# Recurrence outputs with tokens on partitions in a two-layer mixer kernel

## The chip, the cores and the metric

One Trainium2 chip, one of its cores. The metric is the device time in microseconds of one execution: 1113.66 us, median of three runs (1113.42 to 1113.71). PE is the matmul engine, DVE the vector engine, ACT the scalar engine, SP the queue that loads weights.

## What is computed

256 tokens of width 1024 go through two blocks, each with three parallel mixers and a gated feed-forward part. Only three kinds of mixer matter here.

- The gated linear recurrences: GLA in block 1 (4 heads, values of 128), HGRN2 in block 2 (8 heads of 128). For every head `o[t] = sum over s <= t of A[t, s] v[s]`, where A holds the decayed scores. Then each head's output is normed over its 128 value channels and gated: `o * rsqrt(mean(o*o) + eps) * gain * silu(r)`.
- The mLSTM (4 heads, values of 256): `h[t] = sum A[t, s] v[s] / max(|sum A[t, s]|, exp(-m[t]))`, normed over its 256 channels, times a gain and a gate from `LO`.
- All projections are products of the normed activations with streamed weights.

All tensors are fp32. Projections are made in three passes of a rounded type (high part by high part, high by low, low by high).

## The kernel before

Weights come in 170 "pairs" of 128 x 2048 words through three slots. For each pair p SP loads `raw` (the slot is free once the low part is made), ACT rounds it (`whi`, L281), DVE takes the rest (`wlo`, L288), and PE runs 48 matmuls (L306) into accumulator `pp[p % 3]`; ACT or DVE then evacuate it (copies and tanh on ACT, the four-tap convolution begun on ACT at L408 and ended on DVE at L427). The mixers' own work is written by hand between the pairs: each of PE, ACT and DVE has a `Stream`, and `st.go(n)` puts the next n slots there. A slot of PE is one pair. A slot p of ACT or DVE is the split of pair p+2 (it needs pair p-1 done by PE) and the evacuation of pair p-1. All instructions of an engine run in the order written; engines wait for each other by semaphores. PE waits for the low part of a pair (`lo_ready`) and for the evacuation of pair p-3.

Block 1 starts with six slots (W_START) during which the GLA gates are made: logits on ACT (L952), `gated_gates_dve` (L1056), logarithm on ACT (L965, L966), `gated_decay_dve` with the cumulative sums (L1065, L1067). PE needs the sums for the first scores (L908 to L919).

A gated round r (0 GLA, 1 and 2 the two halves of HGRN2) computes scores in nine levels, then the values (L928 to L933): v is the stationary operand and A moves, so that channels lie on partitions and tokens run along the row. The result is copied and squared by ACT (L1017, L1019). Mean squares over channels are then sums over partitions: eight matmuls with one column (`token_sum`, L780), one slot later. ACT takes the root (L1024), DVE the reciprocal and its split in two rounded parts (L793, L794); another slot later sixteen rounded matmuls (`spread_columns`, L787) spread the factor over the partitions, and DVE multiplies (L1148), having put gain and gate in before (L1130, L1133). ACT and DVE write the two parts of Y.

The mLSTM works a head at a time: scores (L1363 to L1367), exponentials (L1416), weights (L1466), their sum over s by one-column matmuls, values with channels on partitions (L1381, L1382) into bank 3 or 4 in turn, copy and square (L1425, L1426), squares over partitions again by one-column matmuls (L1387). After the fourth head DVE joins the factors (L1493 to L1502), PE spreads them (L1392), and DVE multiplies by gain and factor (L1511) and by the gate (L1515).

PSUM: three accumulators `pp`, and five banks `pm` for the mixers.

Of the kernel before, what the change touches and what calls it, by code (L numbers as in the profile page):

```python
# [85 lines left out]
    + [("A", "copyA", LV + j, 4) for j in range(4)]  # L86
# [30 lines left out]
def taken(p):  # L117

    who = {"copy": "act_taken", "tanh": "act_taken", "copyA": "act_taken", "none": None}.get(PAIR[p][1], "dve_taken")
    act = ("copy", "tanh", "copyA")  # L120
    return who, sum((PAIR[x][1] in act) == (who == "act_taken") for x in PAIR if x <= p and PAIR[x][1] != "none")
# [54 lines left out]
def program(nc, ctx, stream, xt, cols, consts, masks, g1w, g2w, poolw, rows_w, rows, gains, out):  # L176
# [31 lines left out]
    SR = sb("SR", [128, 16], F32R)  # L208
# [182 lines left out]
    def evac_act(act, p, spec):  # L391
# [3 lines left out]
        if kind in ("copy", "tanh", "copyA", "conv"):  # L395
            act.wait_ge(pair_done, p + 1)
# [6 lines left out]
        elif kind == "copyA":  # L403
            act.activation(P[:, at:at + arg + 1:arg, :], ps[:, :].rearrange("p (a t) -> p a t", a=2),
                           ACT.Copy).then_inc(S("act_taken"), 1)
        elif kind == "conv":
            for h in range(2):
                act.activation(P[:, at + h, :], ps[:, h * 256:h * 256 + 256], ACT.Identity,  # L408
                               bias=col("conv_b", arg + h), scale=col("conv_w", 72 + arg + h)).then_inc(conv_started, 1)
# [368 lines left out]
    def token_sum(pe, dst, tile, u, first=True, last=True):  # L778

        return pe.matmul(dst, tile[:, u * 128:u * 128 + 128], one, start=first, stop=last, skip_group_check=True)  # L780

    def spread_columns(pe, dst, cols):

        for u in range(2):
            for part in range(2):
                at = 8 * part + cols[u]
                i = pe.matmul(dst[:, u * 128:u * 128 + 128], SR[:, at:at + 1].to_broadcast([128, 128]), CR[:, 0:128],  # L787
                              start=part == 0, stop=part == 1)
        return i

    def round_columns(dve, src):

        link(dve, dve.tensor_copy(SR[:, 0:8], src))  # L793
        return dve.tensor_tensor(SR[:, 8:16], src, SR[:, 0:8].bitcast(F32), ALU.subtract)  # L794

# [87 lines left out]
    def gated_pe(pe, r, st):  # L883
# [42 lines left out]
        o = [pm[:, 1024 + h * 256:1280 + h * 256] for h in range(4)]  # L926
        for h in range(4):
            pe.matmul(o[h][:, 128:256], g["v"](0, h), a_words(g, h)[:, 128:256], start=h % 2 == 0, stop=False, skip_group_check=True)  # L928
        taken_scores(pe, r, 3)
        pe.wait_ge(S("diagonal_spread"), 4 * r + 4)  # L930
        for h in range(4):
            pe.matmul(o[h][:, 0:128], g["v"](0, h), a_words(g, h)[:, 0:128], start=False, stop=True, skip_group_check=True)
            i = pe.matmul(o[h][:, 128:256], g["v"](1, h), a_words(g, h)[:, 256:384], start=False, stop=True, skip_group_check=True)  # L933
        i.then_inc(S("gated_o_ready"), 1)
        st.go(1)
        pe.wait_ge(S("gated_squares"), r + 1)
        for h in range(4):
            for u in range(2):
                i = token_sum(pe, bank(2)[:, 2 * h + u:2 * h + u + 1], HF[:, 4 + h, :], u)
        i.then_inc(S("gated_sums"), 1)  # L940
        st.go(1)
        pe.wait_ge(S("gated_rsqrt"), r + 1)
        pe.wait_ge(S("ident_rounded"), 1)
        for h in range(4):
            i = spread_columns(pe, bank(3 + h // 2)[:, (h % 2) * 256:(h % 2) * 256 + 256], (2 * h, 2 * h + 1))
        i.then_inc(S("gated_norm_spread"), 1)
# [21 lines left out]
    def gated_act(act, r, st):  # L968
# [30 lines left out]
        for n in range(8):  # L999
# [17 lines left out]
        act.activation(P[:, g["o"]:g["o"] + 4, :], pm[:, 1024:2048].rearrange("p (a t) -> p a t", a=4), ACT.Copy)\  # L1017
           .then_inc(S("gated_o_copied"), 1)
# [5 lines left out]
        act.activation(SC[:, 72:80], bank(2)[:, 0:8], ACT.Sqrt, bias=eps4, scale=4.0 / 128).then_inc(S("gated_rms"), 1)  # L1024
# [3 lines left out]
        elif r == 2:  # L1028
            act.wait_ge(S("gated_rsqrt"), 3)
# [44 lines left out]
    def gated_dve(dve, r, st):  # L1074
# [55 lines left out]
        link(dve, dve.scalar_tensor_tensor(GD(g), GD(g), 1.0, P[:, g["r"]:g["r"] + 4, :], ALU.add, ALU.mult))  # L1130
        dve.wait_ge(S("gated_o_copied"), r + 1)
        o = P[:, g["o"]:g["o"] + 4, :]
        link(dve, dve.scalar_tensor_tensor(o, o, col(g["gain"]), GD(g), ALU.mult, ALU.mult))  # L1133
        if r == 1:

            differences(0, gated(2))
        st.go(1)
        dve.wait_ge(S("gated_rms"), r + 1)
        link(dve, dve.reciprocal(SC[:, 80:88], SC[:, 72:80]))
        round_columns(dve, SC[:, 80:88]).then_inc(S("gated_rsqrt"), 1)  # L1140
# [6 lines left out]
        dve.wait_ge(S("gated_norm_spread"), r + 1)  # L1147
        dve.tensor_tensor(o, o, pm[:, 1536:2560].rearrange("p (a t) -> p a t", a=4), ALU.mult).then_inc(S("gated_y_ready"), 1)  # L1148
# [203 lines left out]

    def mlstm_pe(pe, st):
        for h in range(5):
# [15 lines left out]
            if h:  # L1370
                n = h - 1
                w = words(EW, 768 + (n % 2) * 384, 384)
                pe.wait_ge(S("lm_w_added"), n + 1)
                if n >= 2:
                    pe.wait_ge(S("lm_h_copied"), 2 * (n - 1))
                token_sum(pe, bank(2)[:, n:n + 1], w[:, 0:256], 0)
                token_sum(pe, bank(2)[:, 4 + n:5 + n], words(EW, (n % 2) * 384, 128), 0)
                for j in range(2):
                    o = bank(3 + n % 2)[:, j * 256:j * 256 + 256]
                    at = n * 256 + j * 128  # L1380
                    pe.matmul(o, words(LV, at, 128), w[:, 0:256], start=True, stop=False)  # L1381
# [876 lines left out]
```

## Time and profile before

| | |
|---|---|
| median of three runs | 1113.66 us |
| the profiled execution | 1113.65 us |
| its span, first to last instruction | 1111.8 us |
| PE busy | 1097.7 us |
| DVE busy | 750.7 us |
| ACT busy | 608.6 us |
| mean granted clock of PE | 0.998 |
| weights loads, us from issue to landing | 4.8 |

"Busy" counts time in which at least one instruction of the engine runs. Matmuls overlap, so the cost of one on PE is read from the distance between starts. A plain fp32 matmul is shown as two records, a transposition or a rounded matmul as one.

### The profile page before, as it was taken

The numbers are of one execution on the slowest core, as the hardware profiler recorded it, in microseconds if no ns is written. First come the engines' busy times: TensorE is split into PE (matmuls) and PEld (weight loads), VectorE is DVE, ScalarE is ACT, GpSimd is POOL, SyncE is SP. The second block draws the span as 40 slices with busy tenths as digits, with TensorE's granted clock in tenths as the row PEclk, the third lists the DMA queues.
The fourth block names the chain that finished last, engine by engine and source line by source line (L and its number), as shares of the span: only waits on it lengthen the run. The fifth ranks groups of instructions, "written<-read, shape, count | busy, mean of one in ns | idle before, by whom it ended". The sixth has DMA issues, their size and how long they took to land.

```text
span 1111.8 us, 22817 instructions
## 1 busy us (share of the span) xinstructions
PE 1097.7 (99%) x9532; PEld 1050.8 (95%) x9532; DVE 750.7 (68%) x980; ACT 608.6 (55%) x790; POOL 0.2 (0%) x4
## 2 busy tenths in 40 slices
PE   9999999999999999999999999999999999999997
PEld 8899999989999998999999999999999989999997
DVE  6355576677555555689969676866558657777776
ACT  6455456346444444687665555566555446545554
POOL 0000000000000000000000000000000000000000
PEclk9999999999999999999999999999999999999999
DMA  8433344564555555344434443444444545555451
GB/s 308 177 134 139 119 169 169 177 221 146 187 190 189 189 189 182 121 152 153 167 127 140 153 150 141 152 152 152 161 180 152 190 152 174 191 187 189 186 189 39
DMA packets 27113, 184.42 MB, mean 166 GB/s; under 512 B 3080, under 2 KB 3608, under 8 KB 5400
## 3 DMA queue, kind: packets, MB, share of 16 engines
q1 hardware_dynamic: 26456, 181.38, 45.6%
q10 hardware_dynamic: 576, 1.85, 0.5%
q8 instruction: 64, 1.05, 0.4%
q14 instruction: 17, 0.14, 0.0%
HBM read 182.17 MB, written 1.05 MB: 165 GB/s over the span
## 4 chain that ended last, share of the span: by engine, by line
PE 53%; DVE 1%; ACT 1%; issue 1%; ACTq 0%
PE pp L306 41%; PE pm L1733 2%; PE pm L1734 2%; PE pm L1735 2%; PE pm L919 1%; PE pm L389 1%; PE pm L387 1%; PE pm L388 1%; PE pm L1574 1%; PE pm L780 1%; PE pm L787 0%; PE pm L1349 0%; PE pm L1381 0%; DVE P L1067 0%; DVE wlo L288 0%
## 5 line engine op out<-in xcount | busy, mean ns | idle before, releaser
L288 DVE TENSOR_TENSOR wlo<-raw,whi 128x2048 fp32r<-128x2048 f32 x169 | 386.7, 2291 | 188.1 <-ACT whi L281 184.1
L306 PE MATMUL pp<-XH,whi 128*128 128x256 f32 x1696 | 485.5, 286 | 0.9 <-DVE wlo L288 0.5
L306 PE MATMUL pp<-XH,wlo 128*128 128x256 f32 x1696 | 481.3, 284 | 0.0
L306 PE MATMUL pp<-XL,whi 128*128 128x256 f32 x1696 | 481.3, 284 | 0.0
L281 ACT ACTIVATE whi<-raw 128x2048 fp32r<-128x2048 f32 x169 | 322.0, 1909 | 57.1 <-PE pp L306 33.8
L306 PEld LDWEIGHTS pp<-XH,whi 128*128 128x128 f32 x1696 | 326.0, 192 | 5.8 <-issue 2.4
L306 PEld LDWEIGHTS pp<-XL,whi 128*128 128x128 f32 x1696 | 326.1, 192 | 0.7
L306 PEld LDWEIGHTS pp<-XH,wlo 128*128 128x128 f32 x1696 | 326.1, 192 | 0.0
L1787 ACT ACTIVATE Y<-P 128x256 fp32r<-128x256 f32 x44 | 18.4, 418 | 132.6 <-DVE P L1820 132.6
L306 PE MATMUL pp<-Y,whi 128*128 128x256 f32 x480 | 86.9, 283 | 0.0
L306 PEld LDWEIGHTS pp<-Y,whi 128*128 128x128 f32 x480 | 75.2, 192 | 0.0
L1733 PE MATMUL pm<-whi,Y 128*128 128x512 f32 x176 | 68.9, 392 | 0.2 <-DVE Y L1810 0.2
L1734 PE MATMUL pm<-wlo,Y 128*128 128x512 f32 x176 | 68.8, 391 | 0.0
L1735 PE MATMUL pm<-whi,Y 128*128 128x512 f32 x176 | 68.6, 390 | 0.0
L306 PE MATMUL pp<-Y,wlo 128*128 128x256 f32 x240 | 68.0, 283 | 0.0
L306 PE MATMUL pp<-whi,XH 128*128 128x256 f32 x192 | 55.4, 289 | 0.0
L306 PE MATMUL pp<-wlo,XH 128*128 128x256 f32 x192 | 54.4, 283 | 0.0
L306 PE MATMUL pp<-whi,XL 128*128 128x256 f32 x192 | 54.4, 283 | 0.0
L1804 DVE SCALAR_TENSOR_TENSOR P<-pp,PC,P 128x255 f32<-128x255 f32 (+1 forms) x88 | 36.4, 476 | 25.4 <-ACT P L1778 25.4
L306 PEld LDWEIGHTS pp<-Y,wlo 128*128 128x128 f32 x240 | 46.0, 192 | 0.0
L1735 PEld LDWEIGHTS pm<-whi,Y 128*128 128x128 f32 x176 | 33.1, 188 | 7.0
L1733 PEld LDWEIGHTS pm<-whi,Y 128*128 128x128 f32 x176 | 33.1, 188 | 6.9 <-DVE Y L1810 0.6
(321 smaller groups left out, 1300.1 us busy)
## 6 DMA issues: line engine op xcount, KB each, us to landing
raw<-stream SPq DMA_DIRECT2D x169, 1024.0 KB, 4.8
P<-gains ACTq DMA_DIRECT2D x3, 512.0 KB, 3.8
X<-xt SPq DMA_DIRECT2D x2, 512.0 KB, 4.3
raw<-stream SPq DMA_DIRECT2D x2, 512.0 KB, 6.7
out<-P SPq DMA_DIRECT2D x4, 256.0 KB, 2.3
C<-consts SPq DMA_DIRECT2D x1, 345.5 KB, 11.5
P<-rows_w ACTq DMA_DIRECT2D x1, 272.0 KB, 3.4
U<-poolw SPq DMA_DIRECT2D x1, 256.0 KB, 10.5
```

Source lines behind the costliest of these rows:

```text
L281: act.activation(whi[:, slot, :], raw[:, slot, :], ACT.Copy).then_inc(hi_ready, 1)
L288: dve.tensor_tensor(wlo[:, slot, :], raw[:, slot, :], whi[:, slot, :].bitcast(F32), ALU.subtract).then_inc(lo_ready, 1)
L306: done = pe.matmul(dst, a, b, start=first and n == 0, stop=last and n == 2, **kw)
L387: pe.matmul(dst, XH[:, k, t], whi[:, slot, at:at + 512], start=first, stop=False, skip_group_check=True)
L388: pe.matmul(dst, XH[:, k, t], wlo[:, slot, at:at + 512], start=False, stop=False, skip_group_check=True)
L389: return pe.matmul(dst, XL[:, k, t], whi[:, slot, at:at + 512], start=False, stop=last, skip_group_check=True)
L780: return pe.matmul(dst, tile[:, u * 128:u * 128 + 128], one, start=first, stop=last, skip_group_check=True)
L1733: pe.matmul(dst, Y[:, y, t], whi[:, slot, at:at + 512], start=first, stop=False, skip_group_check=True)
L1734: pe.matmul(dst, Y[:, y, t], wlo[:, slot, at:at + 512], start=False, stop=False, skip_group_check=True)
L1735: return pe.matmul(dst, Y[:, 4 + y, t], whi[:, slot, at:at + 512], start=False, stop=last, skip_group_check=True)
L1787: act.activation(Y[:, par, :], pr, ACT.Copy).then_inc(S("hidden_hi"), 1)
L1804: i = dve.scalar_tensor_tensor(c[:, lag:], src[:, 0:256 - lag], fcol("ffn_conv_w", g + (44 * k + off)), c[:, lag:], ALU.mult, ALU.add)
```

## The change

Values of the three gated rounds are computed with A stationary and v moving: tokens on partitions, heads and channels along the row. Squares are then summed along the row by DVE (`tensor_reduce`), the factor is one number a partition, DVE scales from PSUM into SBUF, and eight transpositions turn the result back, two slots after the values; gain and gate come behind. In the mLSTM the values lie in rows of 257 words, the last a one, so that the sum of the weights comes out as column 256; squares are summed by ACT's accumulation; both banks 3 and 4 belong to one head, for its two token halves; DVE scales in SBUF, sixteen transpositions turn back, ACT applies the gain. The root of the mLSTM comes a slot sooner, silu 2 of ACT behind it. At the end, DVE makes the GLA gates one slot sooner. Helpers, their tile SR and the list entries of the new kind "copyV" change accordingly.

```diff
@@ -83,7 +83,7 @@
     + [("B", "conv", LQ + 2 * j, 2 * j) for j in range(4)]
-    + [("A", "copyA", LV + j, 4) for j in range(4)]
+    + [("A", "copyV", LV, j) for j in range(4)]
     + [("B", "conv", XS + 2 * j, 8 + 2 * j) if what == "x" else ("B", "tanh", LO + 2 * j, 0.5) for what, j in SSD_ORDER]
@@ -403,6 +402,8 @@
                            ACT.Copy).then_inc(S("act_taken"), 1)
+        elif kind == "copyV":
+            act.activation(mlstm_values()[:, arg::4, 0:256], ps[:, :].rearrange("p (a t) -> p a t", a=2), ACT.Copy).then_inc(S("act_taken"), 1)
         elif kind == "conv":
@@ -775,24 +776,6 @@
-    def token_sum(pe, dst, tile, u, first=True, last=True):
-        return pe.matmul(dst, tile[:, u * 128:u * 128 + 128], one, start=first, stop=last, skip_group_check=True)
-    def spread_columns(pe, dst, cols):
-        for u in range(2):
-            for part in range(2):
-                at = 8 * part + cols[u]
-                i = pe.matmul(dst[:, u * 128:u * 128 + 128], SR[:, at:at + 1].to_broadcast([128, 128]), CR[:, 0:128],
-                              start=part == 0, stop=part == 1)
-        return i
-    def round_columns(dve, src):
-        link(dve, dve.tensor_copy(SR[:, 0:8], src))
-        return dve.tensor_tensor(SR[:, 8:16], src, SR[:, 0:8].bitcast(F32), ALU.subtract)
@@ -923,27 +906,22 @@
         wait_evac(pe, VALUES[r])
-        o = [pm[:, 1024 + h * 256:1280 + h * 256] for h in range(4)]
+        o = [[pm[:, 1024 + u * 512 + h * 128:1152 + u * 512 + h * 128] for h in range(4)] for u in range(2)]
         for h in range(4):
-            pe.matmul(o[h][:, 128:256], g["v"](0, h), a_words(g, h)[:, 128:256], start=h % 2 == 0, stop=False, skip_group_check=True)
+            pe.matmul(o[1][h], a_words(g, h)[:, 128:256], g["v"](0, h), start=h == 0, stop=False, skip_group_check=True)
         taken_scores(pe, r, 3)
...
         for h in range(4):
-            pe.matmul(o[h][:, 0:128], g["v"](0, h), a_words(g, h)[:, 0:128], start=False, stop=True, skip_group_check=True)
-            i = pe.matmul(o[h][:, 128:256], g["v"](1, h), a_words(g, h)[:, 256:384], start=False, stop=True, skip_group_check=True)
+            pe.matmul(o[0][h], a_words(g, h)[:, 0:128], g["v"](0, h), start=h == 0, stop=True, skip_group_check=True)
+            i = pe.matmul(o[1][h], a_words(g, h)[:, 256:384], g["v"](1, h), start=False, stop=True, skip_group_check=True)
         i.then_inc(S("gated_o_ready"), 1)
-        st.go(1)
-        pe.wait_ge(S("gated_squares"), r + 1)
+        st.go(2)
+        pe.wait_ge(S("gated_o_scaled"), r + 1)
         for h in range(4):
             for u in range(2):
-                i = token_sum(pe, bank(2)[:, 2 * h + u:2 * h + u + 1], HF[:, 4 + h, :], u)
-        i.then_inc(S("gated_sums"), 1)
-        st.go(1)
-        pe.wait_ge(S("gated_rsqrt"), r + 1)
-        pe.wait_ge(S("ident_rounded"), 1)
-        for h in range(4):
-            i = spread_columns(pe, bank(3 + h // 2)[:, (h % 2) * 256:(h % 2) * 256 + 256], (2 * h, 2 * h + 1))
-        i.then_inc(S("gated_norm_spread"), 1)
+                i = pe.transpose(bank(3 + h // 2)[:, (h % 2) * 256 + u * 128:(h % 2) * 256 + u * 128 + 128],
+                                 words(g["o"], u * 512 + h * 128, 128), ident)
+        i.then_inc(S("gated_o_turned"), 1)
@@ -1014,19 +992,17 @@
         act.wait_ge(S("gated_o_ready"), r + 1)
-        act.activation(P[:, g["o"]:g["o"] + 4, :], pm[:, 1024:2048].rearrange("p (a t) -> p a t", a=4), ACT.Copy)\
-           .then_inc(S("gated_o_copied"), 1)
         act.activation(HF[:, 4:8, :], pm[:, 1024:2048].rearrange("p (a t) -> p a t", a=4), ACT.Square)\
...
         act.wait_ge(S("gated_sums"), r + 1)
-        act.activation(SC[:, 72:80], bank(2)[:, 0:8], ACT.Sqrt, bias=eps4, scale=4.0 / 128).then_inc(S("gated_rms"), 1)
+        act.activation(SC[:, 72:80], SC[:, 72:80], ACT.Sqrt, bias=eps4, scale=4.0 / 128).then_inc(S("gated_rms"), 1)
         st.go(1)
...
         elif r == 2:
-            act.wait_ge(S("gated_rsqrt"), 3)
+            act.wait_ge(S("gated_o_scaled"), 3)
             wait_evac(act, LAST_QK)
@@ -1127,25 +1103,28 @@
         dve.wait_ge(S("gated_r_tanh"), r + 1)
-        link(dve, dve.scalar_tensor_tensor(GD(g), GD(g), 1.0, P[:, g["r"]:g["r"] + 4, :], ALU.add, ALU.mult))
-        dve.wait_ge(S("gated_o_copied"), r + 1)
-        o = P[:, g["o"]:g["o"] + 4, :]
-        link(dve, dve.scalar_tensor_tensor(o, o, col(g["gain"]), GD(g), ALU.mult, ALU.mult))
+        gate, o = P[:, g["r"]:g["r"] + 4, :], P[:, g["o"]:g["o"] + 4, :]
+        link(dve, dve.scalar_tensor_tensor(gate, GD(g), 1.0, gate, ALU.add, ALU.mult))
         if r == 1:
...
             differences(0, gated(2))
+        by_head = lambda ap: ap.rearrange("p (n d) -> p n d", n=8)
+        dve.wait_ge(S("gated_squares"), r + 1)
+        dve.tensor_reduce(SC[:, 72:80], by_head(HF[:, 4:8, :].rearrange("p a t -> p (a t)")), AX.X, ALU.add).then_inc(S("gated_sums"), 1)
         st.go(1)
...
         link(dve, dve.reciprocal(SC[:, 80:88], SC[:, 72:80]))
-        round_columns(dve, SC[:, 80:88]).then_inc(S("gated_rsqrt"), 1)
+        dve.tensor_tensor(by_head(words(g["o"], 0, 1024)), by_head(pm[:, 1024:2048]), SC[:, 80:88].unsqueeze(2).to_broadcast([128, 8, 128]),
+                          ALU.mult).then_inc(S("gated_o_scaled"), 1)
         st.go(1)
...
                 dve.scalar_tensor_tensor(x, HF[:, 4 * b:4 * b + 4, :], 1.0, x, ALU.add, ALU.mult).then_inc(S("lm_silu"), 1)
-        dve.wait_ge(S("gated_norm_spread"), r + 1)
-        dve.tensor_tensor(o, o, pm[:, 1536:2560].rearrange("p (a t) -> p a t", a=4), ALU.mult).then_inc(S("gated_y_ready"), 1)
+        dve.wait_ge(S("gated_o_turned"), r + 1)
+        dve.scalar_tensor_tensor(o, pm[:, 1536:2560].rearrange("p (a t) -> p a t", a=4), col(g["gain"]), gate, ALU.mult, ALU.mult)\
+           .then_inc(S("gated_y_ready"), 1)
         if r != 1:
@@ -1350,6 +1329,14 @@
+    def mlstm_values():
+        return words(LV, 0, 8 * 257).rearrange("p (n w) -> p n w", n=8)
+    def mlstm_out():
+        return pm[:, 3 * 512:5 * 512].rearrange("p (u d) -> p u d", u=2)
@@ -1370,27 +1357,26 @@
                 w = words(EW, 768 + (n % 2) * 384, 384)
-                pe.wait_ge(S("lm_w_added"), n + 1)
-                if n >= 2:
-                    pe.wait_ge(S("lm_h_copied"), 2 * (n - 1))
-                token_sum(pe, bank(2)[:, n:n + 1], w[:, 0:256], 0)
-                token_sum(pe, bank(2)[:, 4 + n:5 + n], words(EW, (n % 2) * 384, 128), 0)
-                for j in range(2):
-                    o = bank(3 + n % 2)[:, j * 256:j * 256 + 256]
-                    at = n * 256 + j * 128
-                    pe.matmul(o, words(LV, at, 128), w[:, 0:256], start=True, stop=False)
-                    i = pe.matmul(o[:, 128:256], words(LV + 4, at, 128), w[:, 256:384], start=False, stop=True)
-                i.then_inc(S("lm_h"), 1)
+                v = [mlstm_values()[:, n, :], mlstm_values()[:, 4 + n, :]]
+                o = [mlstm_out()[:, u, 0:257] for u in range(2)]
+                pe.wait_ge(S("lm_w"), 2 * n + 2)
+                pe.wait_ge(S("lm_ones"), 1)
+                if n:
+                    pe.wait_ge(S("lm_h_copied"), 4 * n)
+                pe.matmul(o[0], w[:, 0:128], v[0], start=True, stop=True)
+                pe.matmul(o[1], w[:, 128:256], v[0], start=True, stop=False)
+                pe.matmul(o[1], w[:, 256:384], v[1], start=False, stop=True).then_inc(S("lm_h"), 1)
                 st.go(1)
-                pe.wait_ge(S("lm_squares_added"), n + 1)
+        st.go(1)
+        for h in range(4):
+            if h % 2 == 0:
+                pe.wait_ge(S("lm_h_scaled"), h // 2 + 1)
+            for j in range(2):
                 for u in range(2):
-                    i = token_sum(pe, bank(2)[:, 8 + 4 * u + n:9 + 4 * u + n], P[:, EW + 6, :], u)
-                i.then_inc(S("lm_sums"), 1)
-        st.go(1)
-        pe.wait_ge(S("lm_comb"), 1)
-        for h in range(4):
-            i = spread_columns(pe, pm[:, h * 256:h * 256 + 256], (h, 4 + h))
-        i.then_inc(S("lm_spread"), 1)
+                    at = (2 * h + j) * 256 + u * 128
+                    i = pe.transpose(pm[:, at:at + 128], HF[:, 2 * h + u, j * 128:j * 128 + 128], ident)
+            if h % 2:
+                i.then_inc(S("lm_turned"), 1)
@@ -1410,7 +1396,7 @@
             if h >= 2:
-                act.wait_ge(S("lm_w_added"), h - 1)
+                act.wait_ge(S("lm_w"), 2 * (h - 1))
             for v in range(2):
@@ -1419,11 +1405,18 @@
                 act.wait_ge(S("lm_silu"), 2)
-            else:
-                act.wait_ge(S("lm_sums"), h)
-            o = bank(3 + h % 2).rearrange("p (a t) -> p a t", a=2)
-            act.activation(HF[:, 2 * h:2 * h + 2, :], o, ACT.Copy).then_inc(S("lm_h_copied"), 1)
-            act.activation(P[:, EW + 6:EW + 8, :], o, ACT.Square).then_inc(S("lm_h_copied"), 1)
+            o = mlstm_out()
+            act.activation(HF[:, 2 * h:2 * h + 2, :], o[:, :, 0:256], ACT.Copy).then_inc(S("lm_h_copied"), 1)
+            act.activation(SC[:, 88 + h:93 + h:4], o[:, :, 256], ACT.Copy).then_inc(S("lm_h_copied"), 1)
+            for u in range(2):
+                act.activation(P[:, EW + 6 + u, :], o[:, u, 0:256], ACT.Square, accum_out=SC[:, 96 + 4 * u + h:97 + 4 * u + h])\
+                   .then_inc(S("lm_h_copied"), 1)
+        def gains(b):
+            act.wait_ge(S("lm_turned"), b + 1)
+            t = pm[:, b * 1024:b * 1024 + 1024].rearrange("p (a t) -> p a t", a=4)
+            for j in range(2):
+                act.activation(HF[:, 4 * b + j:4 * b + 4:2, :], t[:, j::2, :], ACT.Copy, scale=col("ml_norm", j)).then_inc(S("lm_gained"), 1)
@@ -1440,13 +1433,14 @@
         copies(3)
-        st.go(1)
-        silu_act(act, 2)
         load_sqrt(act)
...
+        st.go(1)
+        silu_act(act, 2)
         st.go(max(LAST_O_SLOT + 2, W_MLSTM[0] + 10) - st.p)
+        gains(0)
+        gains(1)
         silu_act(act, 3)
@@ -1464,65 +1458,50 @@
                 dve.scalar_tensor_tensor(w[:, at], bank(0)[:, at], 0.25 * 128 ** -0.5, e[:, at], ALU.mult, ALU.mult).then_inc(S("lm_w"), 1)
-            dve.wait_ge(S("lm_w"), 2 * h + 2)
-            dve.tensor_tensor(e[:, 0:128], w[:, 128:256], w[:, 256:384], ALU.add).then_inc(S("lm_w_added"), 1)
-        def squares(h):
-            dve.wait_ge(S("lm_h_copied"), 2 * h + 2)
-            dve.tensor_tensor(P[:, EW + 6, :], P[:, EW + 6, :], P[:, EW + 7, :], ALU.add).then_inc(S("lm_squares_added"), 1)
+        ones = mlstm_values()[:, :, 256:257]
+        dve.memset(ones, 1.0).then_inc(S("lm_ones"), 1)
         st.go(1)
...
         for h in (2, 3):
-            st.go(1)
-            squares(h - 2)
-            st.go(1)
+            st.go(2)
             weights(h)
...
         silu_dve(dve, 1)
-        squares(2)
-        st.go(1)
-        squares(3)
-        st.go(1)
-        dve.wait_ge(S("lm_sums"), 4)
+        st.go(1)
+        dve.wait_ge(S("lm_h_copied"), 16)
         dve.wait_ge(S("exp_minus_m"), 1)
         a, b, c = SC[:, 88:96], SC[:, 96:104], SC[:, 104:112]
-        link(dve, dve.tensor_copy(a, bank(2)[:, 0:8]))
         link(dve, dve.scalar_tensor_tensor(a, a, -1.0, a, ALU.mult, ALU.max))
...
         link(dve, dve.reciprocal(a, a))
-        link(dve, dve.tensor_tensor(b, bank(2)[:, 8:16], a, ALU.mult))
+        link(dve, dve.tensor_tensor(b, b, a, ALU.mult))
         dve.tensor_tensor(b, b, a, ALU.mult).then_inc(S("lm_ms"), 1)
...
         link(dve, dve.tensor_tensor(c, c, a, ALU.mult))
-        round_columns(dve, c).then_inc(S("lm_comb"), 1)
+        by_token = c.rearrange("p (u h) -> p h u", u=2)
+        for b in range(2):
+            t = HF[:, 4 * b:4 * b + 4, :].rearrange("p (h u) d -> p h u d", h=2)
+            dve.tensor_tensor(t, t, by_token[:, 2 * b:2 * b + 2, :].unsqueeze(3).to_broadcast([128, 2, 2, 256]), ALU.mult).then_inc(S("lm_h_scaled"), 1)
+        st.go(1)
         silu_dve(dve, 2)
         st.go(1)
-        dve.wait_ge(S("lm_spread"), 1)
         wait_evac(dve, LAST_O_SLOT, ("act_taken",))
-        def normed(h):
-            for j in range(2):
-                t = HF[:, 2 * h + j, :]
-                link(dve, dve.scalar_tensor_tensor(t, t, col("ml_norm", j), pm[:, h * 256:h * 256 + 256], ALU.mult, ALU.mult))
...
             t = HF[:, 4 * b:4 * b + 4, :]
+            dve.wait_ge(S("lm_gained"), 2 * b + 2)
             dve.scalar_tensor_tensor(t, P[:, LO + 4 * b:LO + 4 * b + 4, :], 1.0, t, ALU.add, ALU.mult).then_inc(S("lm_y"), 1)
...
-        normed(0)
-        normed(1)
+        opened(0)
+        opened(1)
         silu_dve(dve, 3)
-        opened(0)
-        st.go(1)
-        normed(2)
-        normed(3)
-        opened(1)
-        st.go(1)
+        st.go(2)
+        dve.wait_ge(S("mb_silu"), 4)
         for b in range(2):
@@ -2038,7 +2017,7 @@
         gate_lo(dve, G1W[:, :], KT * 16, 1)
-        st.go(4)
+        st.go(3)
         gated_gates_dve(dve, 0)
```

## Rows read from the trace of the kernel before

**Rows 1.** The page's first part: busy us (share of the span) xinstructions
```profile
PE 1097.7 (99%) x9532; PEld 1050.8 (95%) x9532; DVE 750.7 (68%) x980; ACT 608.6 (55%) x790; POOL 0.2 (0%) x4
```

**Rows 2.** PE's waits: us in total, times, longest us
```profile
PE pm L919 <- DVE HF L1067: 2.5, 1, 2.5
```

**Rows 3.** PE's timeline, 50 to 80 us: start us, us, engine line op [idle before]
```profile
53.86 0.75 PE L919 MATMUL pm<-P 64*32 64x32 f32 x64 [2.45 <-DVE HF L1067]
54.53 0.39 PE L306 MATMUL pp<-XH,whi 128*128 128x256 f32 x1
...
61.96 0.71 PE L908 MATMUL pm<-HF 64*128 64x128 f32 x8
62.60 0.39 PE L306 MATMUL pp<-XH,whi 128*128 128x256 f32 x1
...
68.55 0.73 PE L914 MATMUL pm<-HF 64*64 64x64 f32 x16
```

**Rows 4.** Windows: length, busy us (xcount) by engine, granted clock, DMA share, GB/s
```profile
56.00:57.00 1.00, 1.00 (x7) 1.00 (x6) 0.43 (x2) 1.00 (x3) 0.00 (x0) 0.50 0.03 8
```

**Rows 5.** Timelines of ACT and DVE, 42 to 54 us
```profile
42.41 1.28 ACT L965 ACT_TABLE_LOAD   x1
44.15 0.68 DVE L1056 SCALAR_TENSOR_TENSOR HF<-HF 128x512 f32<-128x512 f32 x1
44.87 0.63 ACT L965 ACTIVATE HF<-HF 128x512 f32<-128x512 f32 x1 [1.18 <-DVE HF L1056]
...
49.37 2.29 DVE L288 TENSOR_TENSOR wlo<-raw,whi 128x2048 fp32r<-128x2048 f32 x1 [4.54 <-ACT whi L281]
...
52.30 1.42 DVE L1067 TENSOR_TENSOR_SCAN HF<-SC,HF 128x256 f32<-128x256 f32 x2
```

**Rows 6.** PE's timeline, round 0 and first heads of the mLSTM
```profile
111.13 1.84 PE L780 MATMUL pm<-SC,HF 128*128 128x1 f32 x16
112.84 0.36 PE L306 MATMUL pp<-XH,whi 128*128 128x256 f32 x1
...
118.67 1.90 PE L787 MATMUL pm<-CR,SR 128*128 128x128 f32 x16
120.50 0.93 PE L1174 MATMUL pm<-P 64*128 64x128 f32 x8
...
672.68 0.50 PE L780 MATMUL pm<-SC,P 128*128 128x1 f32 x4
673.05 0.68 PE L1363 MATMUL pm<-P 128*128 128x256 f32 x2
```

**Rows 7.** PE's timeline at the transpositions of the SSD, and the window around them
```profile
745.34 1.15 PE L1555 MATMUL pm<-C,P 128*128 128x128 f32 x8 [0.31 <-ACT P L1599]
746.24 0.60 PE L1349 MATMUL pm<-RF,CR 128*128 128x384 f32 x2
...
744.00:746.00 2.00, 1.69 (x16) 1.38 (x15) 0.85 (x2) 1.60 (x4) 0.00 (x0) 1.00 0.47 197
```

**Rows 8.** DVE's and PE's timelines, 645 to 652 us
```profile
645.47 1.22 DVE L1148 TENSOR_TENSOR P<-P,pm 128x1024 f32<-128x1024 f32 x1 [0.21 <-PE pm L787]
...
648.96 2.42 DVE L427 SCALAR_TENSOR_TENSOR P<-pp,PC,P 128x255 f32<-128x255 f32 x6
...
651.48 0.67 PE L1363 MATMUL pm<-P 128*128 128x256 f32 x2 [0.26 <-issue]
```

**Rows 9.** PE's timeline, the first head's values
```profile
665.53 0.68 PE L1381 MATMUL pm<-P 128*128 128x256 f32 x2
...
666.85 0.37 PE L306 MATMUL pp<-XH,whi 128*128 128x256 f32 x1
```

**Rows 10.** Timelines of ACT, DVE and PE, 704 to 719 us
```profile
704.62 0.60 ACT L1425 ACTIVATE HF<-pm 128x512 f32<-128x512 f32 x1 [4.17 <-PE pm L1382]
...
713.89 0.20 DVE L1500 RECIPROCAL SC<-SC 128x8 f32<-128x8 f32 x1 [0.43 <-ACT SC L1447]
...
718.11 0.34 PE L306 MATMUL pp<-XH,whi 128*128 128x256 f32 x1
```

More of the change, by code:

```diff
@@ L117, in taken @@
 def taken(p):
-    who = {"copy": "act_taken", "tanh": "act_taken", "copyA": "act_taken", "none": None}.get(PAIR[p][1], "dve_taken")
-    act = ("copy", "tanh", "copyA")
+    who = {"copy": "act_taken", "tanh": "act_taken", "copyA": "act_taken", "copyV": "act_taken", "none": None}.get(PAIR[p][1], "dve_taken")
+    act = ("copy", "tanh", "copyA", "copyV")
     return who, sum((PAIR[x][1] in act) == (who == "act_taken") for x in PAIR if x <= p and PAIR[x][1] != "none")
@@ L206, in program @@
     SC = sb("SC", [128, 128])
-    SR = sb("SR", [128, 16], F32R)
     R = sb("R", [36, 7 * T])
@@ L394, in evac_act @@
         ps = pp[p % RING]
-        if kind in ("copy", "tanh", "copyA", "conv"):
+        if kind in ("copy", "tanh", "copyA", "copyV", "conv"):
             act.wait_ge(pair_done, p + 1)
```

## The prediction, made before the result was known

> **What bounds the kernel now.** I read the page's first part: PE is busy for 1097.7 of 1111.8 us, DVE for 68%, ACT for 55% [rows 1]. So an instruction of PE that goes or comes is worth its full issue time, and one of DVE or ACT is worth nothing unless PE ends up waiting for it. Then the waits of PE: the longest by far is one of 2.5 us at L919, for a scan of DVE (L1067) [rows 2]. Then PE's timeline, because matmuls are pipelined: what one costs is the distance from its start to the next start, not its duration. An undisturbed pair of weights tiles (48 matmuls at L306) takes 112.84 to 118.67 = 5.83 us [rows 6]. Last the clock by windows, because a wait of PE can cost more than itself.
>
> **The change part by part.**
>
> *The gates a slot sooner (`st.go(4)` to `st.go(3)`).* PE stands until 53.86 at the first score matmul, idle 2.45 us before it. The pair after it runs from 54.53 to 61.96 = 7.43 us, and the same thing one level later (62.60 to 68.55) takes 5.95 us: 1.48 us more, with nothing waited for inside it [rows 3]. The window 56 to 57 us shows why: granted clock 0.50, the 1.2 GHz level, while the matmuls before the wait ran at 2.4 GHz [rows 4]. PE had just been idle, and no other idle stretch of PE behind the start is longer than 0.5 us. So the wait costs 2.45 + 1.48 = 3.93 us. Is it gone when the gates come a slot sooner? Before, DVE does L1056 at 44.15, after the split of slot 4; ACT, ready since its table load from 42.41, waits 1.18 us for it before the exponential at 44.87 that opens its logarithm; DVE then does its split of slot 5 (49.37) and only behind that the decay, whose scans end at 53.72 [rows 5]. After, DVE takes L1056 behind the split of slot 3, about 37.2, so ACT goes on without that wait: where the logarithm ended at 47.5, it now ends near 46.3. DVE is then free (its slot 4 split ends at 44.2), and subtraction (0.7) and scans (1.4) end near 48.5. PE wants them at 51.4. Cover 2.9 us: I take the whole 3.93. Bounds: 0 if something else holds the logarithm, 3.93. DVE's split of slot 5 moves behind the scans, to 51 at the latest; PE needs that tile after one more pair, at 58, and the first decayed keys for level 1 (before at 57.3) by my count near 55, wanted at 58. Behind it nothing is late.
>
> *The three gated rounds, on PE.* Eight value matmuls with swapped operands stay twelve of 128 columns: nothing. Gone are the eight one-column sums (16 records, 111.13 to 112.84 = 1.71 us) and the sixteen matmuls that spread the norm (118.67 to 120.50 = 1.83 us) [rows 6]. Added are eight transpositions; a row of eight takes 745.34 to 746.24 = 0.90 us [rows 7]. Net 1.71 + 1.83 - 0.90 = 2.64 us a round, 7.92 us for three. The transpositions could cost 0.14 us each as PE's shortest groups do (1.1 us), or as much as a 256-column record at most (1.7 us); the eight next to each other are the nearest row.
>
> *The three rounds, beside PE.* ACT loses a 1.0 us copy. DVE swaps one multiply of 1024 elements, the rounding and a last multiply for a reduction, a multiply from PSUM with a broadcast, and one scalar_tensor_tensor from PSUM; each 1024-element operation of DVE takes 1.2 to 1.3 us (L1148 [rows 8]; bounds for those with a broadcast or a reduction 1.1 and 2.4), so DVE gets 1.2 us more a round. New path for PE: values done, square 1.0, reduction 1.2, table and root behind ACT's slot work, reciprocal, multiply 1.2. In round 1 I count it done 7 us after the values; PE comes for it after two pairs, 11.7 us. Cover over 4 us. [...]
>
> *Tail of round 2.* Here a wait grows. PE's first mLSTM scores (L1363, 651.48) start 0.1 us after DVE's conv taps (L427, 648.96 + 2.42 = 651.38), which stand behind L1148 at 645.47, ACT's copy to Y and the low part [rows 8]. From L1148 to the end of the taps: 5.91 us, and 0.07 more after. Before, PE released L1148. After, PE is there 1.71 + 0.93 = 2.64 us sooner, with arrival at the scores at about 648.6. But DVE must first do the two silus of L1146, which ended 0.21 us before L1148 began; these follow ACT, whose root no longer waits for PE's sums but whose next split waits for PE's pair end, some 2 us sooner than it ran. So they end near 643.3, the taps near 649.3, and PE waits 0.8 instead of 0.3: +0.55 us (bounds 0 and +2).
>
> *mLSTM on PE.* Gone: eight groups of four one-column records, each 672.68 to 673.05 = 0.37 us [rows 6], 2.96 us. Values: before, four records of 256 columns and four of 128, 665.53 to 666.85 = 1.32 us a head [rows 9], 1536 columns; after, six of 257, 1542 columns: nothing. No row shows a row of 257 words, at odd starts: bounds for the four heads -0.3 and +5.1 us (each record twice as long); I take 0, the rate of the same type in rows 9. Spread by sixteen rounded matmuls 1.8 us, sixteen transpositions 1.8 us: nothing. Sum -2.96 us.
>
> *mLSTM, waits.* Both output banks now belong to one head, so values of head n wait until ACT has taken head n-1 (two copies, two squares with sums, about 1.9 us). For heads 1 and 2 two pairs lie between. For head 3 only one (5.83 us): behind values 2 ACT starts at once, since its two silu tanhs ended 2 us before: cover near 4 us. The tail is closer. ACT starts taking head 3 at 704.62 [rows 10], frees PSUM 1.9 us later, loads the root's table (1.5), and DVE's small operations, 0.2 us each (five, about 1.0; L1500 [rows 10]), fit beside that. Root, reciprocal, product: +0.8. Two multiplies of 1024, 2.4 us. Only then comes DVE's split for pair 37 (2.29 us, L288 [rows 5]) and the taps (2.42 us). Counted from 703.8, where ACT then starts: 705.6, 707.3, 707.8, 710.2, then 712.5 for the split and 714.9 for the taps that free the accumulator. PE wants both for the pair that began at 718.11 [rows 10]; it comes at about 717.1 (0.74 less of sums, a little less elsewhere). Cover 2.2 us, the thinnest of the change. The next splits and taps repeat it with 2.3 to 2.5 us. What lm_y needs is done 9 us before PE wants it. So no stall: 0, bounds 0 and 4 us.
>
> *The sum*, against the profiled execution (span 1111.8, its time 1113.65, the median 1113.66: the same): -3.93 - 7.92 - 2.96 + 0.55 = -14.26; 1113.65 - 14.26 = **1099.4 us**.
>
> **A rule against it.** In the trace sixteen transpositions start between 743.99 and 746.24, and the window 744 to 746 has a granted clock of 1.00 [rows 7]. The Trainium skill, "TensorE: Matmul & The Clock Gate", section "Part 4: PE-mode transpose", says that transpositions do not count as PE activity in the way matmuls do, and that the full clock does not engage for them. By that rule four stretches of transpositions could each bring a fall of the clock, 5.9 us; the trace does not agree for a stretch as long as the longest new one, but its neighbours differ, so it stays a rival.
>
> **The rivals.**
> *The late wait at the end of the mLSTM.* For it: DVE and ACT are both held by a chain of seven steps with the splits behind it, and the cover is 2.2 us. Against: no step is far from a row. With a broadcast multiply at 2.4 us instead of 1.2 the chain is 2.4 us longer and its successors too: PE waits 1 to 2 us, and the clock may fall (1.48): about 1102.5.
> *The gates do nothing.* If the logarithm stands behind something else, 3.93 us stay: 1103.3. Against: ACT idled 1.18 us for exactly L1056, and PE for exactly L1067.
> *The transpositions lower the clock.* 4 x 1.48 = 5.92: 1105.3. Against: rows 7.
> *Slower than before: the new waits of PE stall each time.* Seven times PE now comes to a result that has gone through ACT and DVE: three o_scaled, three heads, one lm_h_scaled. If each stalled like the one at 53.86, 7 x 3.93 = 27.5 us come on: 1126.9. It decides from about 2.0 us of cost a wait. For it: the price is in the trace, rows 3. Against: covers of 4 us and more at six of the seven.
> *The 257 columns cost double.* +5.1: 1104.5. Against: nothing but that columns set the distance in all rows.
>
> **How the numbers follow.** Forecast 0.76; late wait 0.09; gates nothing 0.04; clock 0.03; double columns 0.04; slower 0.04. The forecast's own spread is about 2 us to each side (transpositions at 0.09 to 0.14 us, 40 of them; small switches). Below, 1096.5 needs every small wait gone as well; above, 1104.5 takes in the late wait, the gates and the doubled columns, and leaves out the clock and the stalls. A measurement tells 0.2% (2.2 us) from no change: faster 0.94 (all but the last rival and half of mishaps that add up), same 0.02, slower 0.04.
>
> **What would show it.** PE's list of waits without L919 <- L1067, and a granted clock of 1.00 from 50 to 60 us; no groups at L780 and L787; 24 transpositions in the rounds at 0.11 us and 16 in the mLSTM; the first mLSTM scores idle 0.5 to 1 us for DVE; values of a head in 1.3 us; PE busy near 1085 us. Wrong would be: a PE wait for ACT's taking of a head, for the scaled outputs, or for wlo and the taps near the last mLSTM pairs; windows below 1.00 behind transpositions.

## The result and the profile after

The changed kernel takes 1098.93 us (median of four runs, 1098.78 to 1099.03), the kernel before 1113.66 us: 14.7 us less, ratio 0.987 (95% interval 0.985 to 0.989). The forecast was 1099.4, from 1096.5 to 1104.5. The profiled execution took 1098.78 us, its span is 1097.0 us. Most line numbers of after lie lower than those of before, by up to 24.

The page's first part; it answers to [rows 1]. PE is busy 14.0 us less, DVE 2.0 us less, ACT 1.3 us more:

```profile
PE 1083.7 (99%) x9420; PEld 1036.1 (94%) x9420; DVE 748.7 (68%) x961; ACT 609.9 (56%) x807; POOL 0.2 (0%) x4
```

PE's waits of after (total, times, longest). The 2.5 us of [rows 2] are gone; the one at the first mLSTM scores (L1350) has grown from 0.3 us [rows 8] to 1.2. The others are of the start (L733, L321) and of the rounds, not of the change. That at L321, 12 us after the start, was 0.6 us in the trace of before and is 1.1 here; it is 1.1 too in e1 and e3, which touch nothing there, so it differs between executions:

```profile
PE pm L733 <- DVE RF L2008: 1.8, 1, 1.8
PE pm L1350 <- issue: 1.2, 1, 1.2
PE pp L321 <- ACT XH L756: 1.1, 1, 1.1
...
PE pm L915 <- ACT U L992: 0.8, 2, 0.4
```

The first GLA scores and the pair behind them on PE's timeline. Against [rows 3] PE does not wait, and the pair takes 5.94 us (52.30 to 58.24), not 7.43:

```profile
51.61 0.76 PE L902 MATMUL pm<-P 64*32 64x32 f32 x64
52.30 0.39 PE L305 MATMUL pp<-XH,whi 128*128 128x256 f32 x1
...
58.24 0.71 PE L891 MATMUL pm<-HF 64*128 64x128 f32 x8
```

DVE's timeline in the same place ([rows 5]): the gates' scans end at 48.83, before slot 5's split, 2.8 us before PE asks; 2.9 were forecast:

```profile
46.68 0.69 DVE L1041 SCALAR_TENSOR_TENSOR HF<-HF 128x512 f32<-128x512 f32 x1 [2.17 <-ACT HF L944]
47.41 1.42 DVE L1043 TENSOR_TENSOR_SCAN HF<-SC,HF 128x256 f32<-128x256 f32 x2
48.86 2.29 DVE L287 TENSOR_TENSOR wlo<-raw,whi 128x2048 fp32r<-128x2048 f32 x1
```

The window that had a granted clock of 0.50 in [rows 4] (after the busy times: the clock, DMA share, GB/s):

```profile
56.00:57.00 1.00, 1.00 (x11) 1.00 (x10) 0.84 (x2) 0.77 (x3) 0.00 (x0) 1.00 0.00 0
```

Transpositions on PE's timeline, eight in round 0 and sixteen in the mLSTM; here stood the groups of [rows 6]. Eight take 0.96 us here up to the next start (0.79 in round 2), sixteen 1.67 us:

```profile
112.99 1.04 PE L922 MATMUL pm<-C,P 128*128 128x128 f32 x8
113.95 0.93 PE L1153 MATMUL pm<-P 64*128 64x128 f32 x8
...
701.77 1.91 PE L1377 MATMUL pm<-C,HF 128*128 128x128 f32 x16
703.44 0.36 PE L305 MATMUL pp<-XH,whi 128*128 128x256 f32 x1
```

The same moments of PE in both traces give the account. The first decayed scores (61.96 [rows 3], here 58.24) come 3.72 us sooner; the end of round 0 (120.50 [rows 6], 113.95) 6.55; the first mLSTM scores (651.48 [rows 8], 640.48) 11.00; the pair behind the mLSTM's last group (718.11 [rows 10], 703.44) 14.67; the end of the span 14.8. So nearly all of it is won in the stretches that the change touches, and nothing comes back later. Through the start's longer wait PE reached the first scores 0.27 us later than before (its last matmul ahead of them starts at 51.40, before at 51.13); the gates' part is therefore 3.72 + 0.27 = 4.0 us.

### The profile page after: what moved, and what is told of

The parts are those of the page before. It is cut to its first block, busy times and chain, and to the rows that moved or that the text cites. A ratio compares the mean times of both kernels' runs of the same rounds, so it can differ in the third digit from the quotient of the medians.

```text
span 1097.0 us, 22586 instructions
## 1 busy us (share of the span) xinstructions
PE 1083.7 (99%) x9420; PEld 1036.1 (94%) x9420; DVE 748.7 (68%) x961; ACT 609.9 (56%) x807; POOL 0.2 (0%) x4
## 4 chain that ended last, share of the span: by engine, by line
PE 53%; DVE 1%; ACT 1%; issue 1%; ACTq 0%
PE pp L305 41%; PE pm L1713 2%; PE pm L1712 2%; PE pm L1714 2%; PE pm L902 1%; PE pm L388 1%; PE pm L387 1%; PE pm L386 1%; PE pm L1553 1%; PE pm L1328 0%; DVE P L1043 0%; DVE wlo L287 0%; PE pm L747 0%; ACT XH L756 0%; PE pm L915 0%
```

## Experiments

**e1, the gates alone.** The kernel before with one figure changed.

```diff
-        st.go(4)
+        st.go(3)
         gated_gates_dve(dve, 0)
```

> The kernel before with the GLA gates made one slot sooner on DVE and nothing else. Theory (PE's time is its issue time, and the wait at 53.86 us costs its length and the half clock behind it): 2.45 + 1.48 = 3.93 us off, 1109.7 us; no window below 1.00 between 50 and 60 us. Rival, the wait alone counts and the clock falls anyway: 1111.2 us, a window at 0.50 stays. Rival, the sooner gates do nothing: 1113.7 us.

Measured 1109.77 us (1109.59 to 1109.94); before, beside it, 1113.5. So 3.7 us go: more than the wait's 2.45. PE's list has no wait at the gates, and the windows from 50 to 62 us all have a granted clock of 1.00. The rival that counts the wait alone falls, and the one that expects nothing.

**e2, the gates put back into the kernel after.**

```diff
-        st.go(3)
+        st.go(4)
         gated_gates_dve(dve, 0)
```

> The kernel after with the gates put back to their old slot. Theory: the 3.9 us come back whole, since nothing else of the change touches that stretch: 1102.8 us, with a wait of about 2.4 us for the scan and a granted clock of 0.50 behind it. Rival, the gain of the three parts is not a sum and some other part hides the wait: 1099 to 1101 us.

Measured 1102.70 us, 3.8 over the kernel after (four executions: three of 1102.67 to 1102.93, one of 1101.55; e5 below says what such a lower one is). In the profiled one, of the upper three, PE's wait and the half clock are back as before. One line of its waits and one window:

```profile
PE pm L902 <- DVE HF L1043: 2.4, 1, 2.4
```

```profile
56.00:57.00 1.00, 1.00 (x7) 1.00 (x6) 0.06 (x1) 0.99 (x4) 0.00 (x0) 0.50 0.28 115
```

**e3, the wait filled with matmuls.** PE's idle stretch is filled, the gates come as late as before.

```diff
+        idle_passes(pe, RF, 384, 15)
         gated_pe(pe, 0, st)
```

> The kernel before; PE fills the wait before the first GLA scores with 15 rounded matmuls of 384 columns on zeros whose result nobody reads (15 x 0.16 = 2.4 us). The wait stays covered time, so only the clock can change. Theory, PE's idleness lowers the clock: it stays at 1.00, the next pair takes 5.9 instead of 7.4 us, 1112.2 us (-1.5). Rival, the fall of the clock has another cause than the idle stretch: 1113.7 us and a window at 0.50. Should the fill be longer than the wait, PE starts the scores late by the difference.

Measured 1112.54 us (1112.16 to 1113.13), 1.0 less than before beside it, of the 1.5 expected; the interval of the ratio (0.9982 to 1.0002) does not exclude no change. In the trace PE is busy through 52 to 54 us, and the window 56 to 57, at 0.50 before, is at 1.00:

```profile
52.00:54.00 2.00, 2.00 (x13) 1.84 (x11) 1.90 (x4) 0.20 (x1) 0.00 (x0) 1.00 0.43 102
56.00:57.00 1.00, 1.00 (x10) 1.00 (x10) 0.28 (x1) 1.00 (x3) 0.00 (x0) 1.00 0.20 82
```

The fill was a little long: its matmuls lie 0.18 us apart, not 0.16, and the scores start 2.81 us after the last matmul of the pair (51.28 to 54.09), before 2.73. Seven of the ten executions took 1112.16 to 1112.64 us, three 1113.03 to 1113.13. Why those three are longer is open; no trace of one was kept.

**e4, the three gated rounds alone.** All edits of `gated_pe`, `gated_act` and `gated_dve` on the kernel before, of which the core is

```diff
-        pe.wait_ge(S("gated_squares"), r + 1)
...
-        pe.wait_ge(S("gated_rsqrt"), r + 1)
...
+        pe.wait_ge(S("gated_o_scaled"), r + 1)
```

> The kernel before with the three gated rounds alone changed (tokens on partitions, DVE's row sums, eight transpositions); mLSTM and gates as before. Theory: 3 x 2.65 us of PE issue time go, and the wait before the first mLSTM scores grows by 0.9 us as in the trace of after: 1113.66 - 7.95 + 0.9 = 1106.6 us. Rival, part of the gain came from the mLSTM or was given back by it: the sum is off by over 1 us. Rival from the prediction, the wait grows by 0.55 only: 1106.3 us.

Measured 1105.96 us, four executions in two pairs: 1105.19 and 1105.36, 1106.56 and 1106.70. The upper pair is the expected value; why there are two is below. Its trace has the wait of 1.2 us before the first mLSTM scores and the old one of 2.4 us at the gates.

**e5, the mLSTM alone.** All edits of the mLSTM's functions and the kind "copyV" on the kernel before, of which the core is

```diff
-                pe.wait_ge(S("lm_w_added"), n + 1)
...
+                pe.matmul(o[0], w[:, 0:128], v[0], start=True, stop=True)
+                pe.matmul(o[1], w[:, 128:256], v[0], start=True, stop=False)
+                pe.matmul(o[1], w[:, 256:384], v[1], start=False, stop=True).then_inc(S("lm_h"), 1)
```

> The kernel before with the mLSTM alone changed (257-word rows, squares by ACT, sixteen transpositions, the root a slot sooner); rounds and gates as before. Theory by the trace of after: the eight groups of one-column records go with what surrounds them, 3.6 us: 1110.1 us. Rival, the prediction's term: 2.96 us, 1110.7 us. Rival, the new waits of the heads or of the tail show once the rounds are as slow as before: 1112 us or more, and PE waiting for ACT's taking of a head.

Measured 1109.98 us; ten executions, three of 1108.42 to 1108.62 and seven of 1109.76 to 1110.33. The upper group against the kernel before's own upper group (1113.46 to 1113.72): 3.6 less (3.8 by their spans), the theory's figure, not 2.96. PE waits for ACT nowhere in the mLSTM. The profiled execution is one of the lower three, and it shows what they are. Here is its wait at the gates, and the clock behind it:

```profile
PE pm L921 <- DVE HF L1069: 2.4, 1, 2.4
```

```profile
54.00:56.00 2.00, 2.00 (x75) 1.96 (x76) 0.56 (x1) 1.35 (x2) 0.00 (x0) 1.00 0.99 422
56.00:57.00 1.00, 1.00 (x10) 1.00 (x10) 0.31 (x1) 1.00 (x3) 0.00 (x0) 1.00 0.09 33
```

PE idled as long as in the kernel before, but the clock did not fall. The kernel before has the same two levels: of 41 executions run beside these experiments 12 took 1111.9 to 1112.3 us, 27 took 1113.3 to 1113.8 and two 1114.8. All 12 have a mean granted clock of 0.999, all 29 one of 0.996 to 0.998, and the two levels of e2, e4, e5 and e8 part in the same way. Kernels without the idle stretch (e1, e6, e9, after) lie within 0.4 us each. So the half clock is paid in most executions, not in all; the levels are 1.2 to 1.4 us apart, where the trace of before gave 1.48. By the same token one trace at 1.00 does not settle e3. What does is that none of its ten executions reached 1113.3 us, as 29 of the 41 did.

**e6, every transposition four times, on the kernel after.**

```diff
-                i = pe.transpose(...)
+                for _ in range(4):
+                    i = pe.transpose(...)
```

> The kernel after with each of its 40 transpositions made four times (same result). PE then has stretches of 32, 32, 32 and 64 transpositions: 3.6 and 7.2 us with next to nothing else. Theory, transpositions keep the clock up like matmuls and cost 0.11 us each: 120 x 0.11 = 13.2 us more, 1112.1 us, no window below 1.00 behind them. Rival, transpositions do not count as activity: the clock falls in or behind each stretch as behind the wait at 53.86 (1.48 us each, more behind the longest): 1118 us or more, windows at 0.50.

Measured 1111.10 us (1111.04 to 1111.17), 12.3 over the kernel after. With the 24 added in round 2 the transpositions end after DVE's silus: DVE now waits 1.75 us for them and starts L1126 (here L1127) 0.3 us behind them, not 1.1, so PE's wait before the mLSTM scores shrank from 1.2 to 0.4 us; this is also why the time is 1 us under the expected 1112.1. With it a transposition costs (12.3 + 0.8) / 120 = 0.109 us. The windows of the first stretch of 32, of the second half of the 64, and behind that:

```profile
113.00:116.60 3.60, 3.60 (x36) 3.43 (x34) 0.00 (x0) 0.00 (x0) 0.00 (x0) 1.00 0.68 269
712.40:716.00 3.60, 3.60 (x35) 3.60 (x34) 2.92 (x6) 1.26 (x2) 0.00 (x0) 1.00 0.83 291
716.00:720.00 4.00, 4.00 (x36) 4.00 (x35) 2.36 (x2) 3.90 (x4) 0.00 (x0) 1.00 0.00 0
```

The clock stays at 1.00, the 2.4 GHz level, in a stretch of 7 us with nothing but transpositions. The Trainium skill, "TensorE: Matmul & The Clock Gate", section "Part 4: PE-mode transpose", says that transpositions do not let the full clock engage; for the full clock once it is granted these runs do not agree. Whether they could raise it from the half is not shown.

**e7 and e8, DVE later in the mLSTM's tail.** Two (e7) or four (e8) additions of 1024 elements ahead of the scaling; their output is not used.

```diff
+        for _ in range(4):
+            link(dve, dve.tensor_tensor(P[:, EW:EW + 4, :], P[:, EW:EW + 4, :], P[:, EW:EW + 4, :], ALU.add))
         by_token = c.rearrange("p (u h) -> p h u", u=2)
```

> The kernel after with two additions of 1024 elements (2.4 us) on DVE in the tail of the mLSTM, ahead of the scaling; their output is not used. In the trace of after the taps that free the accumulator end at 701.08 us and PE comes for it at 703.44: cover 2.36 us. Theory (PE's bound, cover as read): the cover is just eaten, 0 to 0.3 us at this pair, and the same at the two next splits: 1099.0 to 1099.4 us. Rival, the tail has no cover in truth or several times as much: 1101 or 1098.9 us.

> The same with four additions (4.8 us). Theory: PE waits 4.8 - 2.4 = 2.4 to 2.6 us once before the pair behind the transpositions, the delay is then shared by the pairs behind it, and the clock may fall behind it by the price of 1.48 us: 1101.5 us without, 1103 us with the fall. Rival, the cover is several times as large: 1098.9 us. Rival, each of three splits waits by itself: 1105 us or more.

e7 took 1099.31 us, 0.5 over the kernel after (1098.82 in e0, not run beside it but on another chip, where the kernel before took 0.2 us more; 0 to 0.3 expected), e8 1103.07 (three of 1102.9 to 1103.4, one of 1101.87). In e7 the taps end at 703.70, and PE's next pair starts at 703.75; its sixteen transpositions take 1.87 us up to there, not 1.67:

```profile
701.28 2.42 DVE L428 SCALAR_TENSOR_TENSOR P<-pp,PC,P 128x255 f32<-128x255 f32 x6
```

In e8 PE waits for just these taps, and the clock falls behind the wait:

```profile
PE pp L305 <- DVE P L428: 2.5, 1, 2.5
```

```profile
709.00:710.00 1.00, 1.00 (x7) 1.00 (x6) 1.00 (x3) 0.00 (x0) 0.00 (x0) 0.50 0.00 0
```

So the cover of the tail is what the trace shows, 2.4 us: 2.5 us of delay cost 0.5, the next 2.5 cost 3.8. The execution of 1101.87, 1.3 us below the middle one of the other three and with a mean clock of 0.999 against 0.997 and 0.998, is by these signs the one without the fall; no trace of it was kept. Without the fall the second 2.5 us cost 2.6.

**e9, PE's wait before the mLSTM scores asks for less.** The matmuls read nothing of slots 24 to 26.

```diff
-        wait_evac(pe, W_MLSTM[0] - 1)
+        wait_evac(pe, BLK2 + 23)
         mlstm_pe(pe, st)
```

> The kernel after, but PE's wait before the first mLSTM scores asks for the evacuations up to the mLSTM's values (slot 23 of block 2) and no longer for the conv taps of slot 26, which those matmuls don't read. Theory, the 1.16 us before L1350 are spent for these taps: they go, and the weights splits behind are early enough: 1097.8 us. Rival, the wait moves to the next pair or to the splits, which follow the same taps on DVE: 1098.9 us. Rival, PE is held by the silus of q and k: 1098.9 us as well, the wait stays in its place.

Measured 1097.48 us (1097.35 to 1097.60) against 1098.82 (1098.65 to 1098.86) for the kernel after beside it: 1.3 us less. The trace names no releaser for this wait ("issue"); that it was the taps is shown by its going here. **e0** is that run:

> The kernel after, beside the others on the same chip, as their base: 1098.9 us.

PE's timeline: the scores start at 639.11 without a wait, and so do the second ones:

```profile
639.11 0.60 PE L1350 MATMUL pm<-P 128*128 128x256 f32 x2
...
645.92 0.60 PE L1350 MATMUL pm<-P 128*128 128x256 f32 x2
```

DVE's taps still end at 640.32, and its next split, 642.35 to 644.64, is early enough for the pair at 646.9:

```profile
637.90 2.42 DVE L428 SCALAR_TENSOR_TENSOR P<-pp,PC,P 128x255 f32<-128x255 f32 x6
...
642.35 2.29 DVE L287 TENSOR_TENSOR wlo<-raw,whi 128x2048 fp32r<-128x2048 f32 x1 [1.79 <-ACT whi L280]
```

This is the fastest version, 0.986 of the kernel before (0.985 to 0.988).

## Why the prediction was right, step by step

*PE's issue time is the time.* Right: PE's busy time fell by 14.0 us and its waits (summed over their list) by 0.8, together the 14.8 of the span, and the kernels with one part each (e1 -3.7, e4 -6.9 and e5 -3.6 by the upper groups) add up to -14.2.

*Gates, -3.93.* By the traces -3.72, with PE 0.27 us later than before already when it reaches that place, so -4.0; e1 gave -3.7 and e2 +3.8. That the clock's 1.48 us belong to the wait was the step that decided over a third of this term. That PE's idleness is their cause is shown by four runs together: e1 (no idle stretch) has one level only, no execution of e3 (stretch filled) reaches the upper one, e2 brings both back, and e8 makes wait and fall at another place. The prediction took the fall as certain. It is not: about three executions in ten of the kernel before do without, and what decides it is open. Here luck helped: all four executions of before on record with the result are of the upper level; against the lower one the gain is 13.3 us, not 14.7.

*Three rounds, -7.92.* Right in kind, 0.3 small. Round 0 by the traces 6.55 - 3.72 = 2.8, rounds 1 and 2 with the wait 4.45; with the 0.9 by which the wait grew that is 8.2. Transpositions cost 0.10 to 0.12 us each, e6 0.109. The path through ACT and DVE never held PE.

*Tail of round 2, +0.55.* The step was right, its size too small: the wait is 1.16 us, +0.9. PE's and DVE's timelines:

```profile
632.54 1.03 PE L922 MATMUL pm<-C,P 128*128 128x128 f32 x8
633.33 0.36 PE L305 MATMUL pp<-XH,whi 128*128 128x256 f32 x1
...
640.48 0.67 PE L1350 MATMUL pm<-P 128*128 128x256 f32 x2 [1.16 <-issue]
```

```profile
632.13 2.36 DVE L1124 SCALAR_TENSOR_TENSOR P<-HF,P 128x1024 f32<-128x1024 f32 x2 [0.57 <-ACT HF L1008]
634.41 1.28 DVE L1126 SCALAR_TENSOR_TENSOR P<-pm,PC,P 128x1024 f32<-128x1024 f32 x1
...
637.96 2.42 DVE L428 SCALAR_TENSOR_TENSOR P<-pp,PC,P 128x255 f32<-128x255 f32 x6
```

From L1126 to the end of the taps it is 5.97 us, forecast 5.98. But the silus hold L1126 until 634.41, 1.1 us after the transpositions ended at 633.33; by the forecast's own figures it was 0.7 (silus done at 643.3, transpositions at 648.6 - 6.0 = 642.6). The forecast let ACT start its split some 2 us sooner than the 638.10 of before, at the end of PE's pair. Counted back from the same arrival of PE, it ran 0.5 us later than that: at 627.33, 12.0 us ahead of PE's coming for the scores (639.3), where the forecast had 12.5 (636.1 to 648.6). e9 shows that the wait was for nothing that the matmuls read.

*mLSTM, -2.96.* Mis-sized: -3.67 by the traces (651.48 to 718.11 before, 640.48 to 703.44 after), 3.6 by e5. The values of a head on PE's timeline:

```profile
654.16 0.60 PE L1366 MATMUL pm<-P 128*128 128x257 f32 x2
654.60 0.59 PE L1367 MATMUL pm<-P 128*128 128x257 f32 x2
655.03 0.60 PE L1368 MATMUL pm<-P 128*128 128x257 f32 x2
655.28 0.47 PE L305 MATMUL pp<-XH,whi 128*128 128x256 f32 x1
...
661.22 0.60 PE L1350 MATMUL pm<-P 128*128 128x256 f32 x2
```

The values alone take 1.12 us (654.16 to 655.28), not 1.32; with the pair behind them 7.06 us (654.16 to 661.22), against 7.15 (665.53 to 672.68 [rows 6, 9]). That is 0.09 a head and 0.45 us in all (head 4 has two pairs behind it), where the forecast had 0. Then the groups of one-column matmuls cost more than their own length: in the kernel before the same scores take 1.01 us (658.36 to 659.37) behind a pair, and 1.08 (673.05 to 674.13) behind such a group, because it takes 0.51 us and not 0.44 from their first start to the next:

```profile
658.36 0.60 PE L1363 MATMUL pm<-P 128*128 128x256 f32 x2
658.80 0.38 PE L1364 MATMUL pm<-P 128*128 128x128 f32 x2
...
673.56 0.38 PE L1364 MATMUL pm<-P 128*128 128x128 f32 x2
```

Two such scores make 0.15 us; the first records of the values (665.53) show the same. The eight groups themselves are 3.00 us, and the sixteen transpositions take 1.67 us where the spread took 1.74 (716.37 to 718.11): 3.00 + 0.45 + 0.15 + 0.07 = 3.67. The columns set the distance, 0.43 us for two records of 257, so the rival of doubled columns falls.

*mLSTM, waits: none.* Right, and the margins too. ACT has taken head 2 at 684.80 and PE wants the banks at 688.96: 4.2 us, forecast 4. The tail, of ACT and then of DVE ([rows 10]):

```profile
690.47 0.60 ACT L1409 ACTIVATE HF<-pm 128x512 f32<-128x512 f32 x1 [2.95 <-PE pm L1368]
...
693.40 0.30 ACT L1438 ACTIVATE SC<-SC 128x8 f32<-128x8 f32 x1
```

```profile
694.17 2.36 DVE L1489 TENSOR_TENSOR HF<-HF,SC 128x1024 f32<-128x1024 f32 x2
696.45 2.29 DVE L287 TENSOR_TENSOR wlo<-raw,whi 128x2048 fp32r<-128x2048 f32 x1
698.65 2.43 DVE L428 SCALAR_TENSOR_TENSOR P<-pp,PC,P 128x255 f32<-128x255 f32 x6
```

The taps end at 701.08, PE starts at 703.44: cover 2.36 us, forecast 2.2. e7 and e8 measured it.

*Rivals.* The gates that do nothing fell with e1, the clock that falls with transpositions with e6, the doubled columns with the rows above, and the stalls at each new wait with PE's list of waits, in which none of the seven stands. The late wait in the tail is real as a mechanism (e8) but 2.4 us away.

*The number.* The forecast is 0.5 us above the measured time. By the parts: -4.0 gates, -8.2 rounds, +0.9 tail, -3.7 mLSTM, +0.3 from the start's wait, together -14.7. So the errors of 0.7 and 0.3 us that made the forecast too small were half paid for by the tail and by a wait that the change does not touch; the closeness is in that part luck.

## What to carry to other kernels

Where PE is busy 99% of the span, the gain of a rewrite can be counted from start-to-start distances on PE's timeline, if for each new wait the cover is counted as well: who works for it, and what stands before it on that engine. A wait costs its length plus the half-clock stretch that may follow it: here it followed most waits of 2.4 to 2.5 us and not the one of 1.2 us (in the trace of after the windows from 640 to 648 us are at 1.00). When PE gets shorter, look at waits written wider than what the next matmuls read: such a wait cost 0.3 us before and 1.2 us after. And when a group of matmuls goes, read what stands behind it as well: it may have been slower for standing there.

## What I had not expected

A one-column matmul occupies PE as long as one of 128 columns: 0.107 us a record (1.71 us for sixteen [rows 6]), and 0.11 us for the values of round 0 in the kernel before, two records in 0.22 us:

```profile
104.04 0.39 PE L932 MATMUL pm<-P 128*128 128x128 f32 x2
104.26 0.39 PE L933 MATMUL pm<-P 128*128 128x128 f32 x2
```

So sums over partitions by single columns are no cheaper than transpositions. And the clock's fall behind an idle stretch of 2.4 us is not a fixed cost: the same kernel has it in most executions, and not in others, 1.2 to 1.4 us apart.
